# Grouped and differential attention: one DVE instruction for bias and maximum, scores read from PSUM, transposes ahead of the next scores

## What is computed

```python
def gqa_block_attention(q, k, v):            # 4 query heads, 2 key heads, 64 wide
    logits = einsum('bqgrd,bkgd->bgrqk', qi, k) * d ** -0.5
    probs = softmax(logits)
    return einsum('bgrqk,bkgd->bqgrd', probs, v)

def diff_block_attention(q1, q2, k1, k2, v, lam, rel_bias):   # 4 heads, 32 wide
    p1 = softmax(einsum('bqhd,bkhd->bhqk', q1i, k1) * scale + bias)
    p2 = softmax(einsum('bqhd,bkhd->bhqk', q2i, k2) * scale + bias)
    w = p1 - lam * p2
    return einsum('bhqk,bkhd->bqhd', w, v)
```

## Time and profile before

| | us |
|---|---|
| median of 3 runs | 4469.36 |
| lowest, highest | 4468.59, 4471.97 |
| profiled execution, its own time | 4467.54 |
| its span, first to last instruction | 4465.8 |
| mean granted TensorE clock over the span | 0.912 of full |

### The profile page before, as it was taken

The page is one execution under the profiler, slowest core; times in us unless marked ns, Lnnn a source line. Parts: engine busy times, 40 slices in busy tenths (PEclk is TensorE's granted clock), DMA queues, the critical chain, the costliest instruction groups (busy, mean ns, idle before and its releaser), DMA issues. The chain is left out here.

```text
span 4465.8 us, 46290 instructions
## 1 busy us (share of the span) xinstructions
PE 3794.0 (85%) x17300; PEld 2476.6 (55%) x17300; DVE 1780.6 (40%) x2668; ACT 1269.7 (28%) x1955; POOL 139.8 (3%) x60
## 2 busy tenths in 40 slices
PE   6769999978899979366996999988757798699997
PEld 4557877855688857224875433346523587433334
DVE  5745434177444341756334111133367443311114
ACT  3434433147343221244322000023134332100003
POOL 3500000021000000000000000000000000000000
PEclk8989999989999989667997999999867799799999
DMA  2122222110222321000223899942100121499991
GB/s 113 59 72 83 99 90 81 50 48 16 79 99 80 105 80 48 23 17 18 94 69 123 342 418 410 410 197 71 38 0 17 54 99 54 189 420 412 409 397 47
DMA packets 108849, 617.62 MB, mean 138 GB/s; under 512 B 12310, under 2 KB 12694, under 8 KB 58812
## 3 DMA queue, kind: packets, MB, share of 16 engines
q1 hardware_dynamic: 108732, 616.07, 35.6%
HBM read 612.07 MB, written 3.95 MB: 138 GB/s over the span
## 5 line engine op out<-in xcount | busy, mean ns | idle before, releaser
L325 PE MATMUL PS<-WK_r,RING_r 128*128 128x512 f32 x2096 | 832.2, 397 | 0.0
L323 PE MATMUL PS<-WK_r 128*128 128x512 f32 x1712 | 687.9, 402 | 120.5 <-DVE RING_r L320 67.9
L325 PEld LDWEIGHTS PS<-WK_r,RING_r 128*128 128x128 f32 x2096 | 404.2, 193 | 86.7
L323 PEld LDWEIGHTS PS<-WK_r 128*128 128x128 f32 x1712 | 329.7, 193 | 219.7 <-DVE RING_r L320 78.6
L324 PE MATMUL PS<-HT_r,WK_r 128*128 128x512 f32 (+1 forms) x992 | 395.5, 399 | 0.0
L1944 DVE TENSOR_TENSOR XT<-XT,PS 128x512 f32<-128x512 f32 x128 | 88.0, 687 | 579.2 <-PE PS L1870 579.2
L320 DVE TENSOR_TENSOR RING_r<-RING,WK_r 128x1024 fp32r<-128x1024 f32 x194 | 236.7, 1220 | 73.8 <-ACT WK_r L317 73.8
L325 PE MATMUL PS<-AR_r,RING_r 128*128 128x512 f32 x672 | 263.0, 391 | 0.0
L323 PE MATMUL PS<-AR_r,RING_r 128*128 128x512 f32 x640 | 251.1, 392 | 10.3 <-DVE HT_r L320 10.3
L324 PE MATMUL PS<-AR_r,WK_r 128*128 (+1 forms) x592 | 235.5, 398 | 0.0
L320 DVE TENSOR_TENSOR RING_r<-RING,RING_r 128x1280 fp32r<-128x1280 f32 (+1 forms) x80 | 115.1, 1439 | 291.7 <-ACT RING_r L317 291.7
(11 more groups left out here) (345 smaller groups left out, 5494.2 us busy)
## 6 DMA issues: line engine op xcount, KB each, us to landing
AR<-moe SPq DMA_DIRECT2D x288, 1024.0 KB, 11.1
RING<-moe SPq DMA_DIRECT2D x96, 1024.0 KB, 11.6
RING<-ff_in SPq DMA_DIRECT2D x96, 512.0 KB, 3.4
RING<-branch SPq DMA_DIRECT2D x64, 640.0 KB, 3.8
RING<-ff_out SPq DMA_DIRECT2D x48, 512.0 KB, 3.4
RING<-mix_in SPq DMA_DIRECT2D x32, 512.0 KB, 3.4
RING<-lru_in SPq DMA_DIRECT2D x20, 640.0 KB, 4.8
RING<-ple SPq DMA_DIRECT2D x16, 640.0 KB, 11.5
```

The costliest lines, as they stand in the source:

```text
L323: nc.tensor.matmul(out, r(w_high), r(x_high), start=start, stop=False)
L325: return nc.tensor.matmul(out, r(w_low), r(x_high), start=False, stop=stop)
```

## The change

1. Differential: `mix_project` scales the queries CQ by -1/sqrt(32) while it copies them, so the scores come out negated. The bias table is stored negated (the copy at L2064 becomes a multiplication by -1). shift becomes two `tensor_tensor_reduce` of 128x512, each of which adds the negated bias to one map in PSUM, writes it to SBUF and leaves the row's minimum; exps uses scale -1.
2. Grouped: shift is one maximum over 128x1024 that reads PSUM; there is no copy. exps reads the scores from PSUM and writes SBUF, so score(n+2) now waits for exps(n) there.
3. TensorE's order in both: turn(n), then score(n+2), then values(n-1).
4. The raises by a constant are gone, with direct waits in their place; score(0) and score(1) no longer wait for `maxed`.

```diff
     def att_pe(pe, s, items):
         def score(n):
-            pe.wait_ge(s["maxed"], before + n + 1)
+            if n >= 2:
+                if items[n].bias is None:
+                    pe.wait_ge(s["exped"], 2 * (n - 1))
+                else:
+                    pe.wait_ge(s["maxed"], 2 * (n - 1))
...
         for n in range(len(items)):
+            turn(n)
             if n + 2 < len(items):
                 score(n + 2)
-            turn(n)
             if n:
                 values(n - 1)
...
     att_act, exps:
+                if items[n].bias is None:
+                    ins = nc.scalar.activation(buf, bank(2 * (n % 2) + m), ACT.Exp, bias=NM[n % 3][:, m:m + 1],
+                                               accum_out=RS[n % 3][:, m:m + 1])
+                else:
+                    ins = nc.scalar.activation(buf, buf, ACT.Exp, bias=NM[n % 3][:, m:m + 1], scale=-1.0,
+                                               accum_out=RS[n % 3][:, m:m + 1])
...
     att_dve, shift:
             dve.wait_ge(s["scored"], n + 1)
-            for ins in x.shift(SB[n % 3][:, :, 0:x.width], PS[:, 2 * (n % 2):2 * (n % 2) + 2, 0:x.width]):
-                step.count(ins)
-            step.wait()
-            nc.vector.tensor_reduce(NM[n % 3], SB[n % 3][:, :, 0:x.width], X, ALU.max, negate=True).then_inc(s["maxed"], 1)
+            if items[n].bias is None:
+                nc.vector.tensor_reduce(NM[n % 3], PS[:, 2 * (n % 2):2 * (n % 2) + 2], X, ALU.max, negate=True).then_inc(s["maxed"], 1)
+                return
+            if n >= 3:
+                dve.wait_ge(s["turned"], n - 2)
+            for m in range(2):
+                nc.vector.tensor_tensor_reduce(SB[n % 3][:, m], bank(2 * (n % 2) + m), items[n].bias, 1.0, 3e38,
+                                               ALU.add, ALU.min, NM[n % 3][:, m:m + 1]).then_inc(s["maxed"], 1)
...
     mix_project:
-                    nc.scalar.activation(arc(n), bank(n % 4), ACT.Copy).then_inc(s["free"], 1)
+                    nc.scalar.activation(arc(n), bank(n % 4), ACT.Copy,
+                                         scale=-DIFF_D ** -0.5 if n in (CQ, CQ + 1) else 1.0).then_inc(s["free"], 1)
...
     bias table:
-                nc.vector.tensor_copy(wk(10, 7)[:, n * HALF:(n + 1) * HALF], bank(n % 7, 0, HALF)).then_inc(s["out_copied"], 1)
+                nc.vector.tensor_scalar(wk(10, 7)[:, n * HALF:(n + 1) * HALF], bank(n % 7, 0, HALF), -1.0, None, ALU.mult
+                                        ).then_inc(s["out_copied"], 1)
```

More of the change, by code:

```diff
@@ L708, in build, with __init__, att_pe @@
     class Item:
[L712 to L717, removed]
-        def score(n):
-            pe.wait_ge(s["maxed"], before + n + 1)
+        def __init__(self, scores, bias, weigh, values, outs):
+            self.scores, self.bias, self.weigh, self.values, self.outs = scores, bias, weigh, values, outs
+    def att_pe(pe, s, items):
+        maps = len(items[0].values)
+        def score(n):
+            if n >= 2:
[3 more added lines that the diff above has]
+                    pe.wait_ge(s["maxed"], 2 * (n - 1))
             for m, (q, k) in enumerate(items[n].scores):
-                mm = nc.tensor.matmul(bank(2 * (n % 2) + m, 0, items[n].width), q, k, start=True, stop=True)
+                mm = nc.tensor.matmul(bank(2 * (n % 2) + m), q, k, start=True, stop=True)
             mm.then_inc(s["scored"], 1)
         def turn(n):
[L725 to L728, removed]
+            pe.wait_ge(s["weighed"], maps * (n + 1))
+            if n:
+                pe.wait_ge(s["copied"], n)
             for m in range(maps):
-                for kb in range(len(x.values[m])):
-                    mm = nc.tensor.transpose(bank(6 + m, kb * P, P)[0:x.rows],
-                                             SB[n % 3][:, m, kb * P:kb * P + x.rows], cst("ident"))
+                for kb in range(TT):
+                    mm = nc.tensor.transpose(bank(6 + m, kb * P, P), SB[n % 3][:, m, kb * P:(kb + 1) * P], cst("ident"))
             mm.then_inc(s["turned"], 1)
@@ L736, in values @@
             x = items[n]
-            pe.wait_ge(s["copied"], before + n + 1 + COPIED)
-            blocks = len(x.values[0])
-            for kb in range(blocks):
+            pe.wait_ge(s["copied"], n + 1)
+            for kb in range(TT):
                 for m, out in enumerate(x.outs):
-                    mm = nc.tensor.matmul(out, x.values[m][kb], PT[n % 2][0:x.rows, m, kb * P:kb * P + P],
-                                          start=x.first and kb == 0, stop=x.final and kb == blocks - 1)
+                    mm = nc.tensor.matmul(out, x.values[m][kb], PT[n % 2][:, m, kb * P:kb * P + P],
+                                          start=(kb == 0), stop=(kb == TT - 1))
             mm.then_inc(s["summed_v"], 1)
@@ L790, in att_dve @@
                 shift(n + 1)
-            dve.wait_ge(s["exped"], 2 * (before + n + 1))
+            dve.wait_ge(s["exped"], 2 * (n + 1))
             step(nc.vector.reciprocal(RC[n % 3], RS[n % 3]))
-            for ins in items[n].weigh(step, SB[n % 3][:, :, 0:items[n].width], RC[n % 3], CO[n % 3]):
+            for ins in items[n].weigh(step, SB[n % 3], RC[n % 3], CO[n % 3]):
                 ins.then_inc(s["weighed"], 1)
@@ L1269, in grouped @@
                     halves = [slice(0, 64), slice(64, 128)]
-                    items.append(Item([(ar(AQ + c)[rows, t * P:(t + 1) * P], ar(AK)[rows]) for rows in halves], TOK,
-                                      shift, weigh,
+                    items.append(Item([(ar(AQ + c)[rows, t * P:(t + 1) * P], ar(AK)[rows]) for rows in halves], None, weigh,
                                       [[VM[:, kb, q * 64:q * 64 + 64] for kb in range(TT)] for q in range(2)],
-                                      [bank(4 + c, t * P, P)[rows] for rows in halves], True, True))
+                                      [bank(4 + c, t * P, P)[rows] for rows in halves]))
             @block.sync
@@ L1520, in differential @@
                     for t in range(TT):
[L1521 to L1525, removed]
+                        bias = BIAS[:, h, 3 * P - P * t:3 * P - P * t + TOK]
                         def weigh(step, p, rc, co):
```

64 lines of the change are left out of this document (27 added, 37 removed).

## The result

| | before | after |
|---|---|---|
| median of the runs made side by side | 4470.66 us (4) | 4527.53 us (4) |
| lowest, highest | 4468.59, 4473.90 | 4519.81, 4532.22 |
| ratio after/before, 95% interval | | 1.0125 [1.0107, 1.0142] |
| profiled execution, its span | 4467.54, 4465.8 | 4532.22, 4530.5 |
| mean granted clock over the span | 0.912 | 0.899 |

The changed kernel is slower by 1.25%, some 57 us. The forecast was 4532 us with a range from 4502 to 4547.

The account below looks back on a forecast made before the run. Before, DVE bounds differential at clock 1.00 and TensorE at 0.50; grouped has both near their limit. Differential +48 and grouped +15 give +63 us on 4467.54, 4531, or 4532 us with 1.8 to the median; range 4502 to 4547.

Parts of the forecast that it names:

- The ring: Both attentions: shift, weigh, turn, score pass through DVE and TensorE once per item; at 0.50 differential 6.11 us, grouped 6.30.
- The item at clock 0.50, 6.11 us: Differential: shift 1.22, reciprocal to turn 1.71, turn 1.05, score to next shift 2.13; sum 6.11 us.
- The item at clock 1.00, 4.70 us: Differential: shift 1.22, reciprocal to turn 1.71, turn 0.59, score to shift 1.18; sum 4.70 us, against 3.96 before.
- The clock in differential: Differential: granted clock 0.50 from first item to last, TensorE busy 82%, a gap of 1.1 us each item.
- The third rival: Both attentions: the clock stays up wherever gaps are short, giving 4482 us; chance 0.07.
- Differential's sum: Differential: stage end +24.3 us, in layer 1 +25.8, less 1 a layer for a late clock rise; sum +48 us.
- Grouped's sum: Grouped: items of 6.30 us, then 4.47 once the clock rises; +7.7 us a layer, +15.4 in both.
- The lower end: Grouped: the clock up one item earlier, +5.9 us a layer.
- The maximum from PSUM: Grouped: a maximum reads PSUM as fast as SBUF; difference 0.01 us as lower bound, 0.1 us an item as upper.
- The fused pair: Differential: two fused 128x512 instructions on DVE take 1.22 us to the reciprocal, in place of 2.39.
- The total: Whole kernel: 48 + 15 = +63 us on the profiled 4467.54 is 4531; 4532 us against the median.
- The faster rival: Differential: hand-over vanishes, item 2.93 us, 20 us earlier a layer; grouped gains 1.5 a layer; about 4425 us; chance 0.03.

Follow-up runs that it names:

- experiments 1 and 2: experiment 1, and the kernel before with only turn put ahead of score in TensorE's order: 4596.34 us, ratio 1.0286.
- experiment 4: Kernel after, with one more unused 128x512 matmul behind values(n-1) in differential, items 1 to 14: 4493.89 us, ratio to before 1.0061.
- experiment 1: Kernel after, with score put back ahead of turn in both attentions: 4412.28 us, ratio to before 0.9877.

## Why the prediction was right, point by point

- **The ring.** Right. DVE's idle time of 3.23 us ahead of each shift ends with the score, in all 28 later shifts of both layers' differential, and experiments 1 and 2 show that it comes and goes with the order of TensorE's queue alone.
- **The item at clock 0.50, 6.11 us.** Right, 6.11, with all four terms: 1.23, 1.71, 1.05, 2.12. Shift(2) came 7.79 us behind shift(0); the prediction had 7.8.
- **The item at clock 1.00, 4.70 us.** It does not occur in the kernel after; in experiment 4 it is 4.70 and 4.71.
- **The clock in differential.** Right: 0.50 from the first item to the last. The third rival, a clock that stays up wherever gaps are short, is refuted for this ring: gaps of 1.1 us came with 0.50 over 84 us. That rests on the ring's own rows. The section of the Trainium skill that the prediction named ("TensorE: Matmul & The Clock Gate", "HAM oscillation — how this bites in real kernels") doesn't cover this; the one behind it, "A second HAM failure mode: psum-queue depth-cycling", does tell, of a bf16 kernel, that short idle times between groups of matmuls make the clock go up and down, and would have been the one to weigh. The trace of before agrees with it, with clocks of 1.00 and 0.50 in turn; the kernel after goes beyond it, since the clock did not come up again at all.
- **Differential's sum.** From the issue of the bias DMA to the end it took 104.4 us in place of 81.5, and 104.3 in place of 79.9 in layer 1: +22.9 and +24.5, where the prediction had 23.3 and 24.8. Two small errors cancel. Shift(0) came 8.3 us after the issue and not 7.7 in layer 0 (7.8 for 7.6 in layer 1), when the tables had landed. And the late rise of the clock was there, but larger: turn(14) to the end took 5.9 and 6.3 us where I had 7.8 less 1.
- **Grouped's sum.** The mechanism was right and a size was off. Items of 6.30 and then 4.47 us were forecast and measured. Shift(0) to shift(7) grew by 6.5 and 5.1 us, 11.6 together, where the prediction had 15.4. The term at fault is when the clock rises: I had put it behind shift(4), it came before it, so that shift(4) stood 18.7 us behind shift(0) and not 19.8, and in layer 1 it was 17.1. The lower end, 5.9 us a layer, was the nearer value, and layer 1 fell short of it. A second error hid a part of the first in layer 0: the clock was at 0.50 there from the start, and shift(2) came 7.9 us behind shift(0) and not 7.2. In layer 1 the clock was up for a while among the first items, and it was 6.5.
- **The maximum from PSUM.** 1.22 us against 1.22 over SBUF: the lower bound held. The fused pair took 1.23, for 1.22.
- **The total.** The prediction's +63 us meets +57.9 in the two stretches and +57 between the medians. Its profiled execution of 4532.22 us is on the forecast of 4531 to a microsecond, but by an accident: 6.5 us of it lie in the first stage, which the change does not touch.
- **The faster rival.** It did not happen, but its price was wrong, as experiment 1 shows: 4412 us and not 4425. Most of this is grouped's gain, 5.5 and 6.7 us by the shifts for 1.5 a layer. Differential's price was nearly right, 41.8 us for the 2 x 20 forecast, but partly by luck: an item at clock 1.00 is cheaper than the 2.93 us of the prediction by the hand-over counted on DVE's side, up to 0.14 us, and the first items, at clock 0.50, took more.

What stays open: whether the gap itself or the amount and kind of work around it holds the clock down. TensorE was busy 80% of the time at 0.50 in the kernel after (67.38 of 84 us) and 80% at 1.00 in experiment 4 (40.88 of 51), so a busy share alone does not tell the two apart; what differs is the gap (1.09 against 0.92 us), the added matmul, which works on all 128 rows where a score's work on 32, and the level that the clock had already. The fillers tried do not part these three. A filler that is smaller, or one split in two around the gap, was not tried.

## What to carry to other kernels

When two engines hand work to each other through queues in strict order, write down which step of item n+2 stands behind which step of item n on each queue, and add up the way round: if it is longer than either engine's own work, the queue order sets the pace and making an instruction cheaper doesn't help until the order is mended. Here the rest of the change, the cheaper instructions above all, was worth 55 us in the old order, and the order that came with it cost 113; keeping that rest and the old order gave 4412 us, faster than both kernels. Price such a ring at both granted clocks, since the gaps that it leaves in TensorE's work may themselves decide which one is granted.

## What the runs showed of the hardware that I had not expected

- More work made the kernel faster: 28 unused matmuls brought the clock from 0.50 to 1.00 and saved 34 us (experiment 4).
- In grouped, the clock stayed at 1.00 with TensorE busy 16.56 of 22 us, 75%, less than the 80% at which it stayed at 0.50 in differential (the two windows of the kernel after). Which level is held depends on more than the busy share of the moment.
- exp from PSUM is a little cheaper than in place in SBUF. The source view (lowest, median and highest duration in ns) of the kernel after and then of the kernel before:

```profile
L768 ACT ACTIVATE WK<-PS,SM x32: 678/684/689, 1827.4 to 3295.9; 128x512 f32<-128x512 f32 x32
```

```profile
L760 ACT ACTIVATE WK<-WK,SM x96: 704/711/724, 1822.5 to 3461.4; 128x512 f32<-128x512 f32 x96
```

- The length of the first stage varied by 8.6 us between profiled executions of kernels whose code is the same there. A difference of spans is not a difference of the changed stages.
